# Attention rounds spaced by four projection blocks, in a one-core layer of a hybrid RWKV-7 and attention decoder

## What is computed

```
x = x + 1/2 * SwiGLU_1(rmsnorm(x))
P = rmsnorm(x) @ w_in        # RWKV r|k|v|low ranks, attention q|k|v, gates A|B
A = RWKV-7 time mixing       # decay, removal key kk, delta-rule state, group norm, gate
B = dilated window attention # 12 heads in 3 groups, softmax weighted over the groups
x = x + (sigmoid(gA) * (A @ w_branch_rwkv) + sigmoid(gB) * (B @ w_branch_attn)) @ w_out
x = x + 1/2 * SwiGLU_2(rmsnorm(x))
```

## Time and profile before

| | us |
|---|---|
| median of 3 runs | 2337.95 (2337.09 to 2339.88) |
| the profiled execution | 2340.45 |
| its span, first to last instruction | 2338.6 |
| PE busy in it | 2320.9 (99%) |
| DVE busy | 1458.5 (62%) |
| ACT busy | 982.1 (42%) |
| POOL busy | 87.8 (4%) |

### The profile page before, as it was taken

How to read it: one execution, slowest core, us unless ns; L and a number is a source line. 1 busy time by engine, 2 the same in 40 slices (tenths; PEclk the granted TensorE clock), 3 DMA queues, 4 the chain that set the end, 5 groups by cost and what they waited for, 6 DMA issues and landing times.

```text
span 2338.6 us, 57525 instructions
## 1 busy us (share of the span) xinstructions
PE 2320.9 (99%) x23152; PEld 2293.5 (98%) x23152; DVE 1458.5 (62%) x2000; ACT 982.1 (42%) x1257; POOL 87.8 (4%) x146
## 2 busy tenths in 40 slices
PE   9999999999999999999999999999999999999999
PEld 8999999999999999999989999999999999999999
DVE  6555455555556668878767767766555555545554
ACT  6333333333334544655322446544333333333333
POOL 0000000000002100000000000120000000000000
PEclk9999999999999999999999999999999999999999
DMA  7666567555555656545333637655555555555555
GB/s 241 202 226 214 180 216 245 182 182 183 181 173 170 228 191 203 164 133 194 108 102 115 222 124 216 218 182 180 179 180 184 178 182 183 181 181 182 182 165 172
DMA packets 124081, 428.26 MB, mean 183 GB/s; under 512 B 14488, under 2 KB 20760, under 8 KB 123424
## 3 DMA queue, kind: packets, MB, share of 16 engines
q1 hardware_dynamic: 117504, 393.49, 51.4%
q0 software_dynamic: 6432, 32.64, 4.3%
HBM read 415.21 MB, written 21.33 MB: 187 GB/s over the span
## 4 chain that ended last, share of the span: by engine, by line
PE 92%; DVE 4%; ACT 2%; DVEq 1%; issue 1%; DMA 1%; ACTq 0%; SPq 0%
PE bank L273 29%; PE bank L274 29%; PE bank L275 29%; PE bank L1285 3%; DVE wlo L246 2%; ACT whi L240 1%; DVE kkey L1111 0%; DMA x<-in_x 0%; DVE cum L1123 0%; PE bank L1327 0%; PE bank L1423 0%; DMA raw<-in_weights 0%; DVE mx L1154 0%; ACT rkv L682 0%; PE bank L1648 0%
## 5 line engine op out<-in xcount | busy, mean ns | idle before, releaser
L246 DVE TENSOR_TENSOR wlo<-raw,whi 128x1024 fp32r<-128x1024 f32 (+3 forms) x794 | 913.7, 1155 | 600.9 <-ACT whi L240 598.6
L273 PE MATMUL bank<-hhi,whi 128*128 128x264 f32 x4048 | 1163.9, 288 | 4.2 <-DVE wlo L246 3.9
L240 ACT ACTIVATE whi<-raw 128x1024 fp32r<-128x1024 f32 (+3 forms) x794 | 792.3, 1001 | 869.9 <-PE bank L275 851.3
L274 PE MATMUL bank<-hlo,whi 128*128 128x264 f32 x4048 | 1147.3, 283 | 0.0
L275 PE MATMUL bank<-hhi,wlo 128*128 128x264 f32 x4048 | 1146.0, 283 | 0.0
L273 PEld LDWEIGHTS bank<-hhi,whi 128*128 128x128 f32 x4048 | 762.3, 188 | 13.5 <-DVE wlo L246 4.5
L274 PEld LDWEIGHTS bank<-hlo,whi 128*128 128x128 f32 x4048 | 762.8, 188 | 1.1
L275 PEld LDWEIGHTS bank<-hhi,wlo 128*128 128x128 f32 x4048 | 759.0, 188 | 0.0
L273 PE MATMUL bank<-mhi,whi 128*128 128x264 f32 x1408 | 399.5, 284 | 0.0
L275 PE MATMUL bank<-mhi,wlo 128*128 128x264 f32 x1408 | 398.9, 283 | 0.0
L274 PE MATMUL bank<-mlo,whi 128*128 128x264 f32 x1408 | 398.9, 283 | 0.0
(11 more groups left out here) (269 smaller groups left out, 1646.2 us busy)
## 6 DMA issues: line engine op xcount, KB each, us to landing
raw<-in_weights SPq DMA_DIRECT2D x666, 512.0 KB, 3.3
raw<-in_weights SPq DMA_DIRECT2D x64, 384.0 KB, 3.1
out_skv<-in_cache POOLq DMA_DIRECT2D x16, 512.0 KB, 3.8
raw<-in_weights SPq DMA_DIRECT2D x32, 256.0 KB, 3.2
raw<-in_weights SPq DMA_DIRECT2D x32, 192.0 KB, 2.5
side<-stg POOLq DMA_DIRECT2D x18, 132.0 KB, 4.1
gates<-side POOLq DMA_DIRECT2D x1, 2376.0 KB, 14.9
x<-in_x SPq DMA_DIRECT2D x4, 528.0 KB, 7.0
```

The costliest lines, as they stand in the source:

```text
L240: act.activation(whi[:, u % RING, 0:n], raw[:, u % RING, 0:n], ACT.Copy).then_inc(hi_done, 1)
L246: dve.tensor_tensor(wlo[:, s, 0:n], raw[:, s, 0:n], whi[:, s, 0:n].bitcast(F32), ALU.subtract).then_inc(lo_done, 1)
L273: pe.matmul(bank[:, 0:T], hi, xhi[:, k], start=(k == 0), stop=False)
L274: pe.matmul(bank[:, 0:T], hi, xlo[:, k], start=False, stop=False)
```

## The change

Round r has its scores at block 10 + 4r, exponentials and scaling at 11 + 4r, transposes and copies at 12 + 4r, and values at 13 + 4r, one block ahead of the next scores. Scores wait for the values of the round before to be copied, and the waits of `values` for the next masking go. Removal keys 6 and 7, the decays and the decayed products move to other blocks. The copy `obh` moves from block 23 to 22, and `obl` is made in two halves, at block 23 and in gate block 1, with a drain behind the latter.

```diff
-REMOVAL_AT = {3: 0, 4: 1, 6: 2, 7: 3, 8: 4, 9: 5, 15: 6, 20: 7}
-SUMS_AT = {11: 0, 12: 1, 14: 2, 17: 3, 18: 4, 21: 5, 22: 6, 23: 7}
-DECAYED_AT = {12: 0, 14: 1, 17: 2, 18: 3, 21: 4, 22: 5, 23: 6, 24: 7}
+REMOVAL_AT = {3: 0, 4: 1, 6: 2, 7: 3, 8: 4, 9: 5, 20: 6, 21: 7}
+SUMS_AT = {11: 0, 12: 1, 13: 2, 15: 3, 16: 4, 17: 5, 19: 6, 22: 7}
+DECAYED_AT = {12: 0, 13: 1, 15: 2, 16: 3, 17: 4, 19: 5, 22: 6, 24: 7}
...
-                if 11 <= m <= 17 and m % 3 == 2:
-                    exp_act(m // 3 - 3)
+                if m in (11, 15, 19):
+                    exp_act((m - 11) // 4)
...
-                if 11 <= m <= 17 and m % 3 == 2:
-                    scaled(m // 3 - 3)
+                if m in (11, 15, 19):
+                    scaled((m - 11) // 4)
...
                 for rnd in range(ROUNDS):
-                    if m == 12 + 3 * rnd:
+                    if m == 12 + 4 * rnd:
                         probs_act(rnd)
-                    elif m == 14 + 3 * rnd:
+                    elif m == 13 + 4 * rnd:
                         values_act(rnd)
-                if m == 3 * RT - 1:
+                if m == 3 * RT - 2:
                     act.wait_ge(u_vec, 5)
                     act.drain()
                     act.activation(obh[:], ob, ACT.Copy).then_inc(ob_high, 1)
...
-                    if m == 11 + 3 * rnd:
+                    if m == 11 + 4 * rnd:
                         n = len(heads_of(rnd))
                         dve.wait_ge(exp_done, rnd + 1)
                         dve.reciprocal(rl[:, 0:n], ls[:, 0:n]).then_inc(sum_done, 1)
...
-                    if m == 10 + 3 * rnd:
+                    if m == 10 + 4 * rnd:
                         masked(rnd)
                 if m == 3 * RT - 1:
                     dve.wait_ge(ob_high, 1)
-                    dve.tensor_tensor(obl[:], ob, obh[:].bitcast(F32), ALU.subtract).then_inc(ob_done, 1)
+                    ob_low(0)
...
                     to_spill(n - 1)
+                    ob_low(3)
                 lo("gates", n, 1)
+                if n == 1:
+                    dve.drain()
...
+        def ob_low(j):
+            dve.tensor_tensor(obl[:, j:j + 3], ob[:, j:j + 3], obh[:, j:j + 3].bitcast(F32), ALU.subtract).then_inc(ob_done, 1)
...
-                    if m == 10 + 3 * rnd:
+                    if m == 10 + 4 * rnd:
                         scores(rnd)
-                    elif m == 12 + 3 * rnd:
+                    elif m == 12 + 4 * rnd:
                         probs(rnd)
-                    elif m == 14 + 3 * rnd:
+                    elif m == 13 + 4 * rnd:
                         values(rnd)
...
-            pe.wait_ge(ob_done, 1)
+            pe.wait_ge(ob_done, 2)
...
             else:
-                pe.wait_ge(prob_out, rnd)
-                if rnd > 1:
-                    pe.wait_ge(value_out, rnd - 1)
+                pe.wait_ge(value_out, rnd)
...
         def values(rnd):
             pe.wait_ge(prob_out, rnd + 1)
-            if rnd < 2:
-                pe.wait_ge(score_out, rnd + 2)
-            else:
-                pe.wait_ge(value_out, rnd)
```

## The result

The changed kernel takes 2341.23 us (median of 22 runs, 2339.50 to 2343.23) against 2337.65 for the kernel before (22 runs, 2336.12 to 2340.60). The ratio is 1.0014, with a 95% interval from 1.0008 to 1.0020: slower by 3.6 us, between 1.9 and 4.7. That is clear of zero and small, 0.14%. The forecast was 2339.85, +1.9, within 2335.5 to 2344.5.

The account below looks back on a forecast made before the run. The prediction took the VectorE-ScalarE ring to bound the rkv phase. Low-part halves of 0.9 us each plus 0.1 drain gave +1.9 on the 2337.95 median: 2339.85 us, range 2335.5 to 2344.5.

Parts of the forecast that it names:

- the main mechanism: VectorE and ScalarE bound blocks 11 to the first chunk step; waits taken from TensorE there come back later; net +1.9 us.
- the three signs of being wrong: Block 13 or 17 under 7.5 us; ScalarE or VectorE waiting for TensorE, blocks 12 to 23; wider matmul spacing after second stall.
- the ring: VectorE and ScalarE handing each other weights, shifts and decays, blocks 11 to 23: 98.46 us in the new order against 98.49.
- the low part: Output instruction of 1.78 us, hidden in block 23; split over block 23 and gates block 1, each half adds 0.9 us.
- VectorE's side: Product ak of the first chunk, the last TensorE waits for, ends at 1110.0 instead of 1108.1: +1.9 us.
- first and second stall of TensorE: New waits for ScalarE's scaling before the probabilities of rounds 1 and 2: 3.6 and 4.7 us.
- rival A: TensorE's clock falls in the new stalls, costing 3.7 us after the second: +5.5, 2343.4 us; chance 0.12.
- the stretch: Rkv phase from block 11 to the first chunk step, whose length was to grow by 1.9 us.
- The sum of pieces: Ring length added block by block from VectorE's work in each, blocks 11 to 23: 98.46 us, the same pieces reordered.
- The copy obh ... so I take 0: Moving ScalarE's copy from block 23 to 22, which again holds a scan, was to cost 0.
- The clock column should stay at 1.00: Sign of being right: TensorE's granted clock keeps its upper level, 2.4 GHz, in the changed trace.
- TensorE's side: TensorE's own arrival, counted through both stalls: it asks for the first chunk's masked products at 1110.05.

Follow-up runs that it names:

- x1_warm: Changed kernel with TensorE's two stalls before the probabilities of rounds 1 and 2 filled by 6 and 9 matmuls nobody reads: 2345.52 us.
- x3: Kernel before with only the low part changed: obh copied at block 22, halves at block 23 and gates block 1, and the drain: 2339.61 us.
- x8: Changed kernel with 15 added matmuls in its two stalls, only 8 columns wide instead of 264: 2347.28 us.
- x6: Kernel before with the values of rounds 0 and 1 one block later, removing only the two waits for the masking: 2338.64 us.
- x2: Changed kernel with the eighth scan back at block 23 and the low part one instruction there, without drain: 2342.42 us.
- c2: Changed kernel run once more, unchanged, for its profile alone: span 2339.0 us.
- x7: Changed kernel with only TensorE's second stall filled, by 9 matmuls nobody reads: 2345.49 us.
- x5: Kernel before with ScalarE's decay exponentials moved behind the next block's first rounding: 2331.14 us.

## Why the prediction was right where it was, and wrong where it was

The time lies within the range, and the main mechanism was right, but two of the three signs of being wrong that the prediction named came true: ScalarE waited for TensorE between blocks 12 and 23 (0.31 and 0.19 us; with the stalls filled, in x1_warm, it did not), and the matmuls behind the second stall were spaced wider. Both go back to the clock, the step that failed. Measured from block 11 to the chunk products, in us:

| | forecast | measured |
|---|---|---|
| the ring, blocks 11 to 23, with the first half of the low part | +0.9 | +1.2 (99.69 against 98.49) |
| second half and drain | +1.0 | +1.06 (x3) |
| VectorE's side in all | +1.9 | +2.3 (x1, x8) |
| first and second stall of TensorE | 3.6 and 4.7 | 3.54 and 3.11 |
| a fall of the clock, at the chunk products | 0 (rival A: +3.7) | +0.5 |
| the stretch | +1.9 | +2.77 |
| the time | +1.9 | +3.6 (1.9 to 4.7) |

With the stalls filled, x1_warm shows where TensorE would have come to the second stall with the clock up: the filling starts at 1064.80, in an execution that runs 0.5 us later than the first profile. Against 1069.10 there, the stall would have been 4.8 us long, as forecast (4.7).

- **The ring bounds the stretch: right, and shown from both sides.** 3.5 us of waits taken away alone changed nothing (x6), and 1.74 us taken out of each ring block with a scan made the kernel before 7 us faster and the changed one 10. The sum of pieces held in each block but one: block 20, where VectorE has a gap of 0.43 us without a releaser, took 7.19 instead of 6.84. That is the 0.3 missing in the first line. All seven profiles with rounds four blocks apart have this gap; why, no run shows.
- **The low part: right.** Each half costs what the row for its size says, and the first is free beside a scan.
- **"The copy obh ... so I take 0": right in this order only.** x2 shows 0.8 us in a block without a scan.
- **The stalls before the probabilities: right in place and in the size of the first.** The second was 1.6 us shorter, since the clock fell behind the first and TensorE came later. That fall was swallowed, as the sum said.
- **"The clock column should stay at 1.00": this step failed.** It fell behind both stalls in both profiles. So rival A, which I gave 0.12, is what happens, but its price was mis-sized: 3.7 us were taken from the opening; a fall here lost 1.7 (four microseconds at 0.54 to 0.61), and only 0.5 of the second showed, because TensorE's side had a reserve of about 1 us (its wait of 0.98 for `ak` in x1), where the sum had none. I had counted 1.5 us for groups that take 1.2 to 1.5, and VectorE's side came 0.35 later. With a second fall twice as long, as x2 had it, the stretch was 113.08. That the time stayed so near the forecast is in part luck. The reason against it, that the matmuls behind the 2.01 us wait kept their pace, does not carry far: in x6 the clock fell behind a wait of 2.05, in x3 behind one of 2.08. The Trainium skill, TensorE: Matmul & The Clock Gate, The HAM clock gate, says that an idle array goes to half clock and comes back only after work; the windows agree, with PEclk 0.50 in the middle of a fall.
- **What stays open.** The stretch explains 2.8 of the 3.6 us. The rest is within the interval and was seen in no profile; the part behind the stretch differs by up to 2 us from one execution to the next, in part by its gaps without a releaser. And the later loads of the samples' state on POOL have no wait of TensorE behind them in the trace; they were not tried alone.

## What to carry to other kernels

When two engines feed a third, find out from the waits of all three who waits for whom before pricing a wait on the busiest one: if the feeders wait only for each other, a wait removed from the third comes back later. Look for the instruction that lengthens the feeders' round; here it was two exponentials ahead of a rounding instead of behind it, and moving them was worth 0.3%, with or without the new spacing, where the change as a whole cost 0.14% and the spacing itself gave nothing. An instruction that costs nothing now lies in somebody's wait; before moving it or what makes the wait, name that wait.

## What the runs showed that I had not expected

- In the twelve profiles, from 1000 to 1400, the clock of TensorE fell thirteen times. Ten falls cost about 1.7 us each; three lasted twice as long, began before the stall was over and cost 2.7 to 3.0 (c2, x2, x7). Falls came in or behind waits of 2.05 us (x6), 2.08 (x3) and 2.19 (c2) as well as of 3.5; behind 2.01 us (both profiles of the kernel before) and 2.02 (x3) it did not come. Three falls, at 1284 to 1297 in x1, x5 and x6, had no wait of over 0.7 us in the 35 us before them. What decides stays open.
- 15 added matmuls of 8 columns, in the rkv phase, made the chunk phase slower: the time rose by 6 us. In the one profile taken, TensorE's gaps without a releaser were 6.7 us instead of 1.8. 9 or 15 wide ones, placed where TensorE stood still anyway, added 4 us.
